# A stack of transformer blocks on one Trainium2 core: two weight remainders of the third attention move from VectorE to GpSimd

## The chip, the cores and the metric

The kernel runs on one core of one Trainium2 chip. The metric is the device time of one execution in microseconds (us); lower is better. All engines of the core work side by side and meet at semaphores only: TensorE (PE, with its weight loads shown apart as PEld), VectorE (DVE), ScalarE (ACT), GpSimd (POOL), and SyncE (SP), which only issues DMAs here.

## The reference

One sequence of 256 rows of width 1024 goes through four mixers in turn: stick-breaking attention and a gated conv MLP, forgetting attention and a gated conv MLP, and then the two layers of a second block. What the change touches is the first layer of that second block, a sliding-window attention with 16 query heads over 2 key heads and a gate ("the third attention"):

```python
def attention_mixer(h, positions, w_in, b_in, sinks, w_out, b_out):
    proj = h @ w_in + b_in
    q, k, v, z = jnp.split(proj, [ATTN_WIDTH, ATTN_WIDTH + KV_WIDTH, ATTN_WIDTH + 2 * KV_WIDTH], axis=-1)
    q = partial_rope(q.reshape(B, T, N_HEADS_2, HEAD_DIM_2), positions)
    k = partial_rope(k.reshape(B, T, N_KV_HEADS, HEAD_DIM_2), positions)
    v = v.reshape(B, T, N_KV_HEADS, HEAD_DIM_2)
    o = sliding_window_gqa(q, k, v, sinks)
    return (o * jax.nn.silu(z)) @ w_out + b_out
```

`sliding_window_gqa` is a softmax over a band of 128 keys with one learned sink per head; the layer after it is a gated recurrence. All of it is float32.

## The kernel before

**Weights.** All weight matrices lie in one stream of units, each 128 partitions by 2048 float32 (1 MB). SyncE loads unit after unit into three slots of `raw` (L391 to L397). TensorE multiplies in a rounded float32 format, so each unit is split in two: ScalarE writes the rounded part, `w_hi = round(raw)` (`split_hi`, L553 to L561), and VectorE the remainder, `w_lo = raw - w_hi` (`split_lo`, L1113 to L1117). A product then takes three matmuls, hi by hi, hi by lo and lo by hi (L1942 to L1944). `w_hi` and `w_lo` have three slots each. Four counters tie this together. `hi_done` counts finished rounded parts, `lo_done` finished remainders, `unit_done` the units that TensorE has used up, and `raw_loaded` the loads. SyncE loads unit u only when `lo_done` has reached u - 2, ScalarE rounds unit u only when `unit_done` has reached u - 2, and TensorE starts on unit u when `lo_done` has reached u + 1.

**The third attention.** Counted from zero, unit 98 holds its key and value weights, 99 to 102 its query weights, 103 to 106 the gate weights (`at_z`), 107 to 110 the output weights (`at_o`), and 111 is the first of the recurrence. The stage is written out by hand, one list of steps per engine: `window()` on ScalarE (L887), on VectorE (L1568) and on TensorE (L2569). The 16 heads go in eight pairs p = 0 to 7. For each pair TensorE makes the logits (L2356). VectorE adds the mask and takes the row maximum (`pair_max`, L1455), and makes `nmx` and `esink` from it (L1458, L1460). ScalarE takes the exponentials (L839, L843); VectorE sums and normalizes (`normalize`, L1468 to L1472). TensorE turns the probabilities (L2335), ScalarE copies them out (L852), and TensorE multiplies by the values (L2345, L2347). VectorE applies the gate (`gated`, L1589, after `gate_made`, L1583), and splits the result for the output product (`out_lo`, L1595, after ScalarE's L907). The pieces of the gate and output products lie between these steps on TensorE, so that it has work while a pair goes around the other engines. TensorE's logits of pair p wait for `gated` of pair p - 2, since they share PSUM banks.

VectorE does its remainders in fixed places in its list: unit 104 after the maximum of pair 0, unit 105 after `gated(0)`, 106 after the gate rows of unit 104, 107 after those of unit 105, and so on:

```python
                gated(0)
                split_to(u0 + 3)
...
                normalize(1, 3)
                gate_rows(2)
                split_to(u0 + 5)
```

Here `u0` is 103, so `split_to(u0 + 3)` brings the remainders up to unit 105 and `split_to(u0 + 5)` up to unit 107.

**GpSimd** makes constants and clears masked corners of the first two attentions (`affine_select`, L421). From then on it computes the small reciprocal square roots of the norms (L500, L506) and issues the loads of the norm gains (L494). Before the third attention its list reads `pre_scales(4)`, `next_gain(4)`, `post_scales(4)` (L528 to L530): the last waits for the norm that follows this attention.

Of the kernel before, what the change touches and what calls it, by code (L numbers as in the profile page):

```python
# [21 lines left out]
F32 = mybir.dt.float32  # L22
# [4 lines left out]
ALU = mybir.AluOpType  # L27
# [20 lines left out]
UNIT = 2048  # L48
RAW = 3
HL = 3  # L50
# [13 lines left out]
U0, E0 = {}, {}  # L64
# [24 lines left out]
def build(nc, stream, pvec, post_g, x_in, wf, bf, b_in, b_out, sinks, gnorm, pos, out):  # L89
    with ExitStack() as ctx:  # L90
        def sb(name, shape, dt=F32):
            return ctx.enter_context(nc.sbuf_tensor(name, shape, dt))

        def sem(name):
            return ctx.enter_context(nc.semaphore(name))

        raw = sb("raw", [P, RAW, UNIT])
        w_hi = sb("w_hi", [P, HL, UNIT], F32R)
        w_lo = sb("w_lo", [P, HL, UNIT], F32R)
# [35 lines left out]
        st = sb("st", [P, 12, 9, TT])  # L135
# [22 lines left out]
        last_rows_new = sem("last_rows_new")  # L158
        hi_done = sem("hi_done")
        lo_done = sem("lo_done")  # L160
        unit_done = sem("unit_done")
        chunk_freed_v = sem("chunk_freed_v")
        chunk_freed_s = sem("chunk_freed_s")
# [153 lines left out]
        def rows_wait(i, tt, c):  # L317

            if i in (1, 3):
                done = 2 * tt + c + 1  # L320
                return (rows_done, ROWS0[i] + done) if done < 4 else (unit_done, U0_END[i])
            return (rows_done, ROWS0[i] + c + 1) if tt == 0 else (unit_done, U0_END[i] - 1 + c)

# [89 lines left out]
        def _(pool):  # L413
# [77 lines left out]
            def next_gain(i):  # L491

                pool.wait_ge(h_new, 2 * TT * i)
                pool.dma_start(gbc[:, :], post_g[i].partition_broadcast(P)).then_inc(gbc_loaded, 16)  # L494

            def post_scales(i):

                for tt in range(TT):
                    pool.wait_ge(norm_mean, TT * i + tt + 1)
                    nc.gpsimd.tensor_tensor(st[:, 2 * i + 1, 4, tt:tt + 1], st[:, 2 * i + 1, 3, tt:tt + 1], minus_half[:, 0:1],  # L500
                                            ALU.pow).then_inc(norm_scale, 1)

            def pre_scales(i):

                pool.wait_ge(pre_mean, i + 1)
                nc.gpsimd.tensor_tensor(st[:, 2 * i, 4, :], st[:, 2 * i, 3, :], minus_half[:, :], ALU.pow).then_inc(row_scale, TT)  # L506
# [20 lines left out]
                post_scales(i)  # L527
            pre_scales(4)  # L528
            next_gain(4)
            post_scales(4)  # L530
            pre_scales(5)
            next_gain(5)
# [12 lines left out]
        def _(act):  # L545
# [34 lines left out]
            def split_half(u, i):  # L580

                cols = slice(1024 * i, 1024 * i + 1024)
                if i == 0:
                    assert u == nsplit[0]
                    act.wait_ge(raw_loaded[u % RAW], 16 * whole_loads(u))
                    act.wait_ge(unit_done, u - HL + 1)
                nc.scalar.activation(w_hi[:, u % HL, cols], raw[:, u % RAW, cols], ACT.Copy).then_inc(hi_done if i else half_hi, 1)
                if i:
                    nsplit[0] = u + 1

            def early_quarter(u, q):

                cols = slice(512 * q, 512 * q + 512)
                if u < EARLY:
                    act.wait_ge(quarter_loaded[4 * u + q], 16)
                elif q == 0:
                    act.wait_ge(raw_loaded[u % RAW], 16 * whole_loads(u))
                nc.scalar.activation(w_hi[:, u, cols], raw[:, u, cols], ACT.Copy).then_inc(hi_done if q == 3 else quarter_hi, 1)
                nsplit[0] = u + 1
# [9 lines left out]
            def pre(n, gain):  # L609


                for b in range(4):
                    if n % 2 and b == 1:
                        pre_square(n, 0, 1)
                    if n in SECOND and b in (1, 2):
                        pre_square(n, 1, b - 1)
# [8 lines left out]
                    if n == 0:  # L625
                        early_quarter(0, b)
                    if n in SECOND and b in (1, 2):
                        split_half(SECOND[n], b - 1)

            def pre_square(n, tt, c):  # L630

                if n == 0:
                    act.wait_ge(x_loaded[tt], 16)
                else:
                    act.wait_ge(h_new, 2 * TT * (n - 1) + 2 * tt + c + 1)
                nc.scalar.activation(junk(tt, c), h[:, tt, 512 * c:512 * c + 512], ACT.Square, scale=D ** -0.5,
                                     accum_out=st[:, 2 * n, c, tt:tt + 1]).then_inc(norm_ss, 1)
# [458 lines left out]
        def _(dve):  # L1096
# [8 lines left out]
            V = nc.vector  # L1105
# [7 lines left out]
            def split_lo(u, slot, raw_slot):  # L1113

                dve.wait_ge(hi_done, u + 1)
                V.tensor_tensor(w_lo[:, slot, :], raw[:, raw_slot, :], w_hi[:, slot, :].bitcast(F32),  # L1116
                                ALU.subtract).then_inc(lo_done, 1)  # L1117

            def split_to(n):
                for u in range(nsplit[0], min(n, NU)):  # L1120
                    split_lo(u, u % HL, u % RAW)
                nsplit[0] = max(nsplit[0], min(n, NU))

            def split_quarter(u, q):
# [9 lines left out]
            def split_half(u, i):  # L1134

                cols = slice(1024 * i, 1024 * i + 1024)
                if i:
                    dve.wait_ge(hi_done, u + 1)
                else:
                    assert u == nsplit[0]  # L1140
                    dve.wait_ge(half_hi, HALVED.index(u) + 1)
                V.tensor_tensor(w_lo[:, u % HL, cols], raw[:, u % RAW, cols], w_hi[:, u % HL, cols].bitcast(F32),
                                ALU.subtract).then_inc(lo_done if i else half_lo, 1)
                if i:
                    nsplit[0] = u + 1

            def early_quarter(u, q):

                cols = slice(512 * q, 512 * q + 512)
                if q == 3:  # L1150
                    dve.wait_ge(hi_done, u + 1)
                else:
                    dve.wait_ge(quarter_hi, 3 * u + q + 1)
                V.tensor_tensor(w_lo[:, u, cols], raw[:, u, cols], w_hi[:, u, cols].bitcast(F32),
                                ALU.subtract).then_inc(lo_done if q == 3 else quarter_lo, 1)
                nsplit[0] = u + 1
# [14 lines left out]
            def pre(n, gain):  # L1171
                for b in range(4):

                    if n in SECOND and b == 2:
                        pre_means(n)
# [6 lines left out]
                    if n == 0:  # L1182
                        early_quarter(0, b)
                    if n in SECOND and b in (1, 2):
                        split_half(SECOND[n], b - 1)

# [15 lines left out]
            def pre_means(n):  # L1202

                stats = st[:, 2 * n]
                dve.wait_ge(norm_ss, squares(2 * n, 1, 1))
                V.scalar_tensor_tensor(stats[:, 3, :], stats[:, 0, :], EPS, stats[:, 1, :], ALU.add, ALU.add).then_inc(pre_mean, 1)
# [94 lines left out]
            def conv_ffn(layer):  # L1301
# [45 lines left out]
                def chunk(j):  # L1347
                    if j < NJ - 1:
                        split_to(u0 + 3 * j + (3 if j else 4))
                    scaled(j, u0 + 3 * j + (2 if j == 0 else 0 if j == NJ - 1 else 1), j == 0)  # L1350
                    taps(j, j % 2)
                    if j < NJ - 1:
                        split_to(u0 + 3 * j + 4)
                    product(j, j % 2)
                    if j < NJ - 1:
                        split_to(u0 + 3 * j + 5)
                    if j == NJ - 1:
                        split_to(u0 + 3 * NJ)
                    gate_lo(j, j % 2)
# [1465 lines left out]


ROWS0 = [0, 2, 5, 7, 10, 12]
SECOND = {1: U0["ffn0"] + 1, 2: U0["fox_q"] + 1, 3: U0["ffn1"] + 1, 5: U0["rec_f"] + 1}
HALVED = list(SECOND.values())

# [78 lines left out]
```

## Time and profile before

| | |
|---|---|
| median of 3 runs | 866.98 us (866.67 to 867.33) |
| profiled execution, its own time | 867.6 us |
| its span in the trace | 865.9 us |
| PE busy | 854.0 us, 99% of the span |
| PEld busy | 751.9 us, 87% |
| DVE busy | 677.9 us, 78% |
| ACT busy | 524.0 us, 61% |
| POOL busy | 65.1 us, 8% |
| granted clock of TensorE | 0.999, mean over the span |

The profiled execution took 867.6 us, 0.6 us over the median of the three runs; its records cover 865.9 us of it, and the remaining 1.7 us lie around them. The third attention with its output product lies at about 640 to 720 us from the start of the span.

### The profile page before, as it was taken

What the parts mean: (1) busy time and instruction counts of PE and PEld (TensorE: products, weight loads), DVE (VectorE), ACT (ScalarE), POOL (GpSimd) and SP (SyncE); (2) the same over time, 40 slices, a digit from 0 to 9 for tenths busy, and PEclk for the clock granted to TensorE, in tenths of its full rate; (3) what the DMA queues carried; (4) which work ended last, traced back from release to release, by engine and by line L of the source; (5) the groups of instructions that cost most, each with busy time, mean ns of one, the idle gap of its engine ahead of it and who ended that gap; (6) DMA issues with size and microseconds to landing.
All of it is one profiled execution on the core that took longest, in us unless ns stands there. A gap on an engine that the chain in (4) does not pass through costs nothing.

```text
span 865.9 us, 15051 instructions
## 1 busy us (share of the span) xinstructions
PE 854.0 (99%) x5782; PEld 751.9 (87%) x5782; DVE 677.9 (78%) x994; ACT 524.0 (61%) x766; POOL 65.1 (8%) x128
## 2 busy tenths in 40 slices
PE   8999999999999999999999999999999999999997
PEld 8999889888888889999898888888888868998885
DVE  5767559897887987566589878888888877699774
ACT  6656557765665674667486655656746857542552
POOL 2354100000000010010010000000000001000010
PEclk9999999999999999999999999999999999999999
DMA  8545335645546445323456455455263244452511
GB/s 296 192 148 188 115 129 189 225 177 212 194 151 232 151 167 199 144 100 131 162 207 241 148 204 204 174 183 206 98 219 137 108 146 129 188 202 95 193 50 48
DMA packets 21976, 144.62 MB, mean 167 GB/s; under 512 B 2831, under 2 KB 3103, under 8 KB 5280
## 3 DMA queue, kind: packets, MB, share of 16 engines
q1 hardware_dynamic: 20448, 139.47, 44.5%
q0 software_dynamic: 1328, 4.32, 1.7%
q8 instruction: 40, 0.66, 0.3%
q14 instruction: 16, 0.13, 0.0%
q10 hardware_dynamic: 144, 0.04, 0.0%
HBM read 142.78 MB, written 1.05 MB: 166 GB/s over the span
## 4 chain that ended last, share of the span: by engine, by line
PE 86%; DVE 8%; ACT 2%; issue 2%; DMA 1%; POOL 0%; DVEq 0%; POOLq 0%; SPq 0%
PE psC L2034 15%; PE psC L1942 11%; PE psC L1944 11%; PE psC L1943 11%; PE psC L2037 8%; PE psD L1942 5%; PE psD L1944 5%; PE psD L1943 5%; DVE w_lo L1116 2%; PE psC L2064 2%; PE psC L2066 2%; PE psC L2073 2%; DVE arena L1330 2%; PE psD L2356 1%; PE psD L2736 1%
## 5 line engine op out<-in xcount | busy, mean ns | idle before, releaser
L1116 DVE TENSOR_TENSOR w_lo<-raw,w_hi 128x2048 fp32r<-128x2048 f32 x125 | 285.8, 2287 | 52.8 <-ACT w_hi L561 52.0
L561 ACT ACTIVATE w_hi<-raw 128x2048 fp32r<-128x2048 f32 x125 | 238.4, 1911 | 66.5 <-PE psC L1944 30.7
L2034 PE MATMUL psC<-xT,w_hi 128*128 128x512 f32 x640 | 200.8, 395 | 0.0
L2037 PEld LDWEIGHTS psC<-xT,w_lo 128*128 128x128 f32 x640 | 120.2, 188 | 28.3
L2037 PE MATMUL psC<-xT,w_lo 128*128 128x256 f32 x640 | 125.7, 278 | 0.0
L2034 PEld LDWEIGHTS psC<-xT,w_hi 128*128 128x128 f32 x640 | 98.6, 189 | 1.2
L1942 PE MATMUL psC<-xT,w_hi 128*128 128x256 f32 x320 | 91.6, 286 | 0.0
L1943 PE MATMUL psC<-xT,w_hi 128*128 128x256 f32 x320 | 90.5, 283 | 0.0
L1944 PE MATMUL psC<-xT,w_lo 128*128 128x256 f32 x320 | 90.5, 283 | 0.0
L1942 PE MATMUL psD<-w_hi,oT_hi 128*128 128x512 f32 x208 | 81.3, 391 | 0.6 <-DVE oT_lo L1344 0.6
L1943 PE MATMUL psD<-w_lo,oT_hi 128*128 128x512 f32 x208 | 81.0, 390 | 0.0
L1944 PE MATMUL psD<-w_hi,oT_lo 128*128 128x512 f32 x208 | 81.0, 389 | 0.0
L1330 DVE SCALAR_TENSOR_TENSOR arena<-arena,pv 128x254 f32<-128x254 f32 (+1 forms) x176 | 75.2, 479 | 5.4 <-DVE arena L1330 1.8
L1942 PE MATMUL psC<-w_hi,xT 128*128 128x256 f32 (+1 forms) x216 | 72.9, 338 | 0.9 <-issue 0.6
L1944 PE MATMUL psC<-w_hi,xT 128*128 128x256 f32 (+1 forms) x216 | 70.5, 327 | 0.0
L1943 PE MATMUL psC<-w_lo,xT 128*128 128x256 f32 (+1 forms) x216 | 70.5, 326 | 0.0
L706 ACT ACTIVATE arena<-arena,pv 128x256 f32<-128x256 f32 x88 | 47.8, 593 | 24.5 <-DVE arena L1320 24.5
L1942 PEld LDWEIGHTS psC<-xT,w_hi 128*128 128x128 f32 x320 | 61.3, 192 | 1.0 <-issue 1.0
L1943 PEld LDWEIGHTS psC<-xT,w_hi 128*128 128x128 f32 x320 | 61.3, 192 | 0.0
L1944 PEld LDWEIGHTS psC<-xT,w_lo 128*128 128x128 f32 x320 | 61.3, 192 | 0.0
L718 ACT ACTIVATE arena<-psC 128x512 f32<-128x512 f32 x40 | 23.8, 596 | 51.5 <-PE psC L2037 51.5
L1942 PEld LDWEIGHTS psC<-w_hi,xT 128*128 128x128 f32 x216 | 41.0, 190 | 6.7 <-issue 2.1
(338 smaller groups left out, 1538.0 us busy)
## 6 DMA issues: line engine op xcount, KB each, us to landing
raw<-stream SPq DMA_DIRECT2D x130, 1024.0 KB, 4.8
gbc<-post_g POOLq DMA_DIRECT2D x6, 512.0 KB, 4.7
h<-x_in SPq DMA_DIRECT2D x2, 512.0 KB, 4.4
raw<-stream SPq DMA_DIRECT2D x4, 256.0 KB, 6.2
out<-h SPq DMA_DIRECT2D x3, 256.0 KB, 2.0
arena<-b_in POOLq DMA_DIRECT2D x1, 640.0 KB, 5.9
out<-h SPq DMA_DIRECT2D x2, 128.0 KB, 2.0
pv<-pvec POOLq DMA_DIRECT2D x1, 176.0 KB, 4.7
```

What stands on the lines that cost most here:

```text
L561: nc.scalar.activation(w_hi[:, slot, :], raw[:, raw_slot, :], ACT.Copy).then_inc(hi_done, 1)
L706: ins = nc.scalar.activation(cv[:, par, g, a, :], xs[:, g, a, :], ACT.Identity, scale=pv[:, bass.ds(at + 2, 1)], bias=pv[:, bass.ds(at + 3 ...
L718: nc.scalar.activation(x_low[:, g], psC[:, at:at + 2, T:2 * T], ACT.Copy).then_inc(f["lower"], 1)
L1116: V.tensor_tensor(w_lo[:, slot, :], raw[:, raw_slot, :], w_hi[:, slot, :].bitcast(F32), ALU.subtract).then_inc(lo_done, 1)
L1330: ins = V.scalar_tensor_tensor(y, xs[:, g, a, 0:T - back], pv[:, bass.ds(at + 2 - back, 1)], y, ALU.mult, ALU.add)
L1942: MM(out, lhs[0], rhs[0], start=start, stop=False, skip_group_check=True)
L1943: MM(out, lhs[0], rhs[1], start=False, stop=False, skip_group_check=True)
L1944: return MM(out, lhs[1], rhs[0], start=False, stop=stop, skip_group_check=True)
L2034: MM(psC[:, up_bank(e, a), :], hi[:, k, a * P:a * P + P], xT[:, kk_, :, :].rearrange("p i t -> p (i t)"), start=(kk_ == 0), stop=False, sk ...
L2037: ins = MM(psC[:, up_bank(e, a), 0:T], lo[:, k, a * P:a * P + P], xT[:, kk_, 0, :], start=False, stop=(kk_ == KT - 1), skip_group_check=True)
L2064: MM(out(a), hi[:, k, a * P:a * P + P], xt[0][:, kk_, :], start=(kk_ == 0 and a % 2 == 0), stop=False, skip_group_check=True)
L2066: MM(out(a), lo[:, k, a * P:a * P + P], xt[0][:, kk_, :], start=False, stop=False, skip_group_check=True)
```

## The change

GpSimd gets two units of weight remainders, 105 (the third gate unit) and 107 (the first output unit). It waits for `hi_done` of the unit and then subtracts in eight operations of 256 columns. The last one counts up a new semaphore, `pool_lo`. VectorE no longer subtracts for these two units: at the same places in its list it waits for `pool_lo` and counts up `lo_done` with a memset of two columns of `st` that nothing else uses. TensorE, SyncE and ScalarE have the lists they had.

```diff
+        pool_lo = sem("pool_lo")
...
             pre_scales(4)
             next_gain(4)
+            for u in POOL_LO:
+                pool.wait_ge(hi_done, u + 1)
+                for at in range(0, UNIT, 256):
+                    cols = slice(at, at + 256)
+                    ins = nc.gpsimd.tensor_tensor(w_lo[:, u % HL, cols], raw[:, u % RAW, cols], w_hi[:, u % HL, cols].bitcast(F32),
+                                                  ALU.subtract)
+                ins.then_inc(pool_lo, 1)
             post_scales(4)
...
             def split_to(n):
                 for u in range(nsplit[0], min(n, NU)):
-                    split_lo(u, u % HL, u % RAW)
+                    if u in POOL_LO:
+                        dve.wait_ge(pool_lo, POOL_LO.index(u) + 1)
+                        V.memset(st[:, POOL_LO.index(u), 2, :], 0.0).then_inc(lo_done, 1)
+                    else:
+                        split_lo(u, u % HL, u % RAW)
                 nsplit[0] = max(nsplit[0], min(n, NU))
...
 ROWS0 = [0, 2, 5, 7, 10, 12]
+POOL_LO = [U0["at_z"] + 2, U0["at_z"] + 4]
```

Two places in the lists of the engines show it. Line numbers of the changed kernel are higher, by one in GpSimd's part before the insertion and by 12 in VectorE's part behind `split_to`. The first place is GpSimd's list between the norm ahead of the third attention and the one behind it. Before:

```order
L506 TENSOR_TENSOR st<-st,minus_half 128x2 [waits pre_mean]
L494 DMA gbc<-post_g 128x1024 [waits h_new]
L500 TENSOR_TENSOR st<-st,minus_half 128x1 [waits norm_mean] x2
L506 TENSOR_TENSOR st<-st,minus_half 128x2 [waits pre_mean]
L494 DMA gbc<-post_g 128x1024 [waits h_new]
```

and now:

```order
L507 TENSOR_TENSOR st<-st,minus_half 128x2 [waits pre_mean]
L495 DMA gbc<-post_g 128x1024 [waits h_new]
L535 TENSOR_TENSOR w_lo<-raw,w_hi 128x256 [waits hi_done]
L535 TENSOR_TENSOR w_lo<-raw,w_hi 128x256 x7
L535 TENSOR_TENSOR w_lo<-raw,w_hi 128x256 [waits hi_done]
L535 TENSOR_TENSOR w_lo<-raw,w_hi 128x256 x7
L501 TENSOR_TENSOR st<-st,minus_half 128x1 [waits norm_mean] x2
```

Sixteen operations stand where GpSimd went straight to the wait for the next norm.

The second place is VectorE's list from the exponentials of pair 1 to the maximum of pair 2. Before:

```order
L1468 TENSOR_TENSOR sums<-sums,esink 128x4 [waits win_exp]
L1469 RECIPROCAL rsum<-sums 128x4 [waits dve_step]
L1472 TENSOR_TENSOR arena<-arena,rsum 128x2x128 [waits dve_step]
L1472 TENSOR_TENSOR arena<-arena,rsum 128x2x256
L1583 SCALAR_TENSOR_TENSOR hn<-arena,hn 128x512 [waits gate_tanh]
L1589 SCALAR_TENSOR_TENSOR arena<-psD,hn 128x256 [waits gate_made,win_out]
L1116 TENSOR_TENSOR w_lo<-raw,w_hi 128x2048 [waits hi_done]
L1455 ISA arena,mx<-psD,mask_window 128x128 [waits win_logit]
```

and now:

```order
L1480 TENSOR_TENSOR sums<-sums,esink 128x4 [waits win_exp]
L1481 RECIPROCAL rsum<-sums 128x4 [waits dve_step]
L1484 TENSOR_TENSOR arena<-arena,rsum 128x2x128 [waits dve_step]
L1484 TENSOR_TENSOR arena<-arena,rsum 128x2x256
L1595 SCALAR_TENSOR_TENSOR hn<-arena,hn 128x512 [waits gate_tanh]
L1601 SCALAR_TENSOR_TENSOR arena<-psD,hn 128x256 [waits gate_made,win_out]
L1131 MEMSET st 128x2 [waits pool_lo]
L1467 ISA arena,mx<-psD,mask_window 128x128 [waits win_logit]
```

The subtraction of 2048 columns has become a memset of two behind a wait for GpSimd; nothing else has moved. Unit 107 is the same exchange, between the gate rows of unit 105 and the maximum of pair 4.

## Rows read from the trace of the kernel before

**Rows 1.** Busy time, share of the span and instructions, from the page's first part.
```profile
PE 854.0 (99%) x5782; PEld 751.9 (87%) x5782; DVE 677.9 (78%) x994; ACT 524.0 (61%) x766; POOL 65.1 (8%) x128
```

**Rows 2.** Busy time by stretch: the sum from 652 to 722 us, then the mean.
```profile
sum 70.00, PE 69.06 PEld 55.28 DVE 58.36 ACT 45.68 POOL 1.10; mean PE 17.27 PEld 13.82 DVE 14.59 ACT 11.42 POOL 0.28
```

**Rows 3.** Timeline of PE: start, us, engine, line, operation, tiles, [idle before and releaser].
```profile
665.14 0.38 PE L2356 MATMUL psD<-kT,qT 64*128 64x128 f32 x2 [0.50 <-DVE arena L1589]
```

**Rows 4.** Chain that ended last, in order of time: start, us, what.
```profile
653.85 2.20 DVE w_lo L1116
656.36 1.03 DVE arena L1472 x2
...
664.65 0.44 DVE arena L1589
```

**Rows 5.** Timeline of DVE between the maximum and the normalizing of pair 0.
```profile
652.17 0.16 DVE L1458 SCALAR_TENSOR_TENSOR nmx<-mx,arena 128x4 f32<-128x4 f32 x1
652.36 0.16 DVE L1460 TENSOR_TENSOR esink<-nmx,arena 128x4 f32<-128x4 f32 x1
652.44 1.40 DVE L1548 SCALAR_TENSOR_TENSOR arena<-psC,st,arena 128x512 f32<-128x512 f32 x2
...
655.96 0.15 DVE L1468 TENSOR_TENSOR sums<-sums,esink 128x4 f32<-128x4 f32 x1
```

**Rows 6.** Timeline of ACT: the rounded parts of units 105 and 107.
```profile
650.13 1.91 ACT L561 ACTIVATE w_hi<-raw 128x2048 fp32r<-128x2048 f32 x1 [3.93 <-PE psC L1944]
...
670.69 1.90 ACT L561 ACTIVATE w_hi<-raw 128x2048 fp32r<-128x2048 f32 x1
```

**Rows 7.** Timeline of DVE: the remainders of units 105 and 107.
```profile
665.00 2.28 DVE L1116 TENSOR_TENSOR w_lo<-raw,w_hi 128x2048 fp32r<-128x2048 f32 x1
...
680.79 2.29 DVE L1116 TENSOR_TENSOR w_lo<-raw,w_hi 128x2048 fp32r<-128x2048 f32 x1
```

**Rows 8.** Timeline of POOL: its last record before the third attention and the next.
```profile
628.84 0.59 POOL L494 DMA_DIRECT2D gbc<-post_g  x1
718.46 0.56 POOL L500 TENSOR_TENSOR st<-st,minus_half 128x1 f32<-128x1 f32 x1 [89.03 <-DVE st L1169]
```

**Rows 9.** Groups of POOL by form: count, busy us, mean ns, idle before and releasers.
```profile
L421 POOL TENSOR_SCALAR_AFFINE_SELECT arena<-arena 128x256 f32<-128x256 f32 x48 | 19.0, 425 | 130.7 <-ACT arena L829 78.4 <-DVE arena L1401 34.2 <-ACT arena L792 18.1
...
L421 POOL TENSOR_SCALAR_AFFINE_SELECT arena<-arena 128x2048 f32<-128x2048 f32 x2 | 4.0, 2004 | 0.1
```

**Rows 10.** DVE and POOL side by side: two lines' shortest, median and longest ns; timelines.
```profile
L1411 DVE CAST oT_hi<-arena x6: 559/648/740, 30.5 to 83.1; 128x768 fp32r<-128x768 f32 x6
...
L1412 DVE TENSOR_TENSOR oT_lo<-arena,oT_hi x6: 958/996/1039, 31.1 to 83.9; 128x768 fp32r<-128x768 f32 x6
...
48.55 0.69 DVE L1418 TENSOR_TENSOR oT_lo<-psC,oT_hi 128x512 fp32r<-128x512 f32 x1 [4.27 <-ACT oT_hi L797]
49.16 2.28 DVE L1116 TENSOR_TENSOR w_lo<-raw,w_hi 128x2048 fp32r<-128x2048 f32 x1
...
49.26 2.34 POOL L421 TENSOR_SCALAR_AFFINE_SELECT mask_level<-mask_level 128x64 int8<-128x64 int8 x1
...
83.00 0.41 POOL L421 TENSOR_SCALAR_AFFINE_SELECT arena<-arena 128x256 f32<-128x256 f32 x1
...
83.36 0.72 POOL L421 TENSOR_SCALAR_AFFINE_SELECT arena<-arena 128x256 f32<-128x256 f32 x1
...
83.08 0.74 DVE L1411 CAST oT_hi<-arena 128x768 fp32r<-128x768 f32 x1 [0.87 <-POOL arena L421]
83.86 1.04 DVE L1412 TENSOR_TENSOR oT_lo<-arena,oT_hi 128x768 fp32r<-128x768 f32 x1
```

**Rows 11.** Around unit 107: DVE normalizing pair 3, PE turning pair 3, PE's last wait.
```profile
679.12 1.03 DVE L1472 TENSOR_TENSOR arena<-arena,rsum 128x256 f32<-128x256 f32 x2
...
682.77 0.87 PE L2335 MATMUL psD<-ident,arena 128*128 128x128 f32 x6
...
705.26 0.87 PE L2335 MATMUL psD<-ident,arena 128*128 128x128 f32 x6 [0.42 <-DVE arena L1472]
```

## The prediction

> **What bounds the kernel now.** The page's first part comes first: PE is busy for 854.0 us, 99% of the span, VectorE for 78% and GpSimd for 8% [rows 1]. A cheaper VectorE can only give back time in which PE stands still. So the next view is the busy time by stretch: from 652 to 722 us, the 70 us in which the two units are split and used, PE is busy for 69.06 [rows 2]. Its idle time there is 0.94 us. The timeline of PE shows where most of it is. 0.50 us lie ahead of the logits of pair 2 at 665.14, which wait for VectorE's `gated(0)` (L1589) [rows 3]. 0.42 us lie ahead of the turning of pair 6 at 705.26, which waits for VectorE's normalizing [rows 11].
>
> The chain of work that ended last says more about the first of these. Between 652 and 665 us it doesn't run over PE but over VectorE: the remainder of unit 104, the normalizing of pair 0, and at last `gated(0)` at 664.65, which lets PE go on [rows 4]. In that stretch VectorE has no slack at all, and whatever delays it delays the end.
>
> When do the new operations run? GpSimd has nothing to do between 629.4 and 718.46 [rows 8], so it starts on a unit as soon as ScalarE has rounded it. For unit 105 that is 650.13 + 1.91 = 652.04, and for unit 107 it is 670.69 + 1.90 = 672.59 [rows 6]. VectorE comes to them only at 665.00 and 680.79 [rows 7]. The first eight operations thus fall exactly into the stretch in which VectorE carries the chain.
>
> **What is taken away.** Two subtractions of 2.28 and 2.29 us leave VectorE [rows 7]. Both lie behind `gated(0)`, so neither shortens the way to 665.14. What can come out of them is at most PE's idle time behind that point, 0.94 - 0.50 = 0.44 us [rows 2, 3]. Nearly all of it is the 0.42 at 705.26. Behind unit 107 VectorE's list waits for PE's logits of pairs 4, 5 and 6 in turn, so what it gained has gone by then, and between the last of these and 705.26 stands the remainder of unit 110, which VectorE keeps. I cost this relief at 0. The two memsets that replace the subtractions are two columns wide; they cost nothing on PE's path.
>
> **What an operation on GpSimd costs.** No row shows a two-input subtraction there. The nearest are operations with one input: 0.41 us for 256 columns alone, 0.36 from one start to the next (83.00 to 83.36) [rows 10], and 2.00 us for 2048 [rows 9]. That is (2.00 - 0.41) / 1792 = 0.89 ns for a column. If the second input is read after the first, it adds 256 x 0.89 ns = 0.23 us, which makes 0.59 from start to start and 4.7 us for a unit. The lower bound is the one-input spacing, 0.36; the upper is two one-input operations one after the other, 0.77 with the first alone. I take 0.59, between them, because it scales the same loop by the data it has to read.
>
> The Trainium skill, GPSIMD Engine Reference, section "Performance versus the Vector engine", gives 4497 ns for a 2048-column float32 `tensor_tensor` on GpSimd and says to keep elementwise work on VectorE. By it an eighth would be 0.56 us and the result below some 0.2 us smaller; no run so far shows the figure.
>
> **What the two engines do to each other.** Rows 10 have it in both directions. VectorE's cast (L1411) takes 559 ns undisturbed, and 740 where it starts at 83.08, inside GpSimd's operation of 83.00. GpSimd's next one, issued at 83.36, then takes 0.72 us instead of 0.41: it had to let the cast finish. VectorE's subtraction behind it (L1412, two inputs in SBUF) takes 1.04 instead of 0.96. And a small GpSimd operation that starts at 49.26, 0.10 us into a remainder of 2.28 us, lasts 2.34 us. So one of them stands still until the other's whole instruction is over. A VectorE instruction with one input from PSUM isn't touched: L1418 takes 0.69 us in the midst of GpSimd's mask operations [rows 10].
>
> The Trainium skill, SBUF — State Buffer, section "Who interferes with whom", has this as a rule: a VectorE instruction with two SBUF inputs and a GpSimd instruction that reads SBUF shut each other out for a whole instruction. By this rule GpSimd's subtractions aren't work beside VectorE's but partly in front of it; the rows above agree.
>
> **The sum for unit 105.** GpSimd starts at 652.1 and runs an operation every 0.59 us, and I let the two engines take turns. From each wait I take off 0.1 us, because the waits in rows 10 (0.18 and 0.08 us) are that much shorter than the overlap of the records. VectorE's instructions with two SBUF inputs are met in this order [rows 4, 5]:
> - `nmx` at 652.17 waits for the first operation: 0.4.
> - `esink`, which comes after it through a semaphore, waits for the second: 0.45.
> - The two L1548 read PSUM and run free for 1.3 us, while operations 3 to 5 pass.
> - The remainder of unit 104 (653.76) meets one of them half way: 0.3. GpSimd stands still for its 2.28 us.
> - `sums` (655.96) finds the sixth operation in front: 0.5.
> - The two L1472 (656.36) meet the seventh and eighth: 0.25 and 0.45.
>
> That is 2.35 us, say 2.4, and the eight operations end near 659.5, in time for 665. The whole delay goes through. The maximum of pair 1, ScalarE's exponentials and tanh, `gate_made(0)` and `gated(0)` follow one on another, and PE, which already waits 0.50 us there, starts the logits of pair 2 2.4 us later. Behind it PE is bound by its own work, so nothing is won back. With a spacing of 0.36 the same walk gives 0.7 us, with 0.77 it gives 3.6.
>
> **The sum for unit 107.** Here VectorE has room. PE turns pair 3 at 682.77, and the normalizing that it needs ends at 679.12 + 1.03 = 680.15 [rows 11], 2.6 us earlier; the missing remainder of unit 105 adds some 0.6, as pair 3's maximum no longer starts behind PE's logits. Eight collisions cost some 2.3 us, spread over instructions of which only some stand ahead of that point. I cost them at 0; at 0.77 us an operation they could reach 4, and cost PE up to 1. GpSimd needs 4.7 us and the 2.28 of unit 106's remainder, until 679.6, and VectorE asks at about 680.8, so the new wait isn't the later one.
>
> **Sum**: 0 + 2.4 + 0 = +2.4 us. Against the profiled execution of 867.6 that is 870.0; against the median of the runs, 866.98, which lies 0.6 lower, it is 869.4.
>
> **Rivals.** A measurement of this kernel can tell about 0.2%, 1.7 us, from no change.
> - *GpSimd yields.* If VectorE's next instruction goes first whenever both wait, or if an operation takes only 0.36 us, the small instructions lose 0.1 or 0.2 us each instead of 0.45. The delay is then 0.7 to 1.6 us, and the time 867.7 to 868.6: no change that can be told. This decides below a delay of 1.7 us. For it speaks the one-input spacing; against it speaks that `nmx` and `esink` come one by one through semaphores, so that GpSimd finds a gap each time. 0.28.
> - *The relief pays.* If the engines hardly met and the relief reached 705.26, PE would win up to 0.44 us: 866.5. Faster by over 1.7 us would need more than all 0.94 us of idle time in the stretch [rows 2]. 0.03 for that.
> - *Unit 107 hurts too.* With operations of 0.77 us the first unit costs 3.6 and the second up to 1: 871.6. If one took over (665.07 - 652.1) / 8 = 1.6 us, VectorE would also wait for `pool_lo`, and the time would pass 875. It lies within the chance for slower, with 0.15.
>
> **How the numbers follow.** The forecast has 0.54 and the worse rival 0.15, so slower by over 0.2% has 0.69, within it 0.28, faster 0.03. The predicted time is that of the likeliest case, 869.4. The range goes from 867.2, which takes in most of the first rival, to 871.8, the two upper bounds together. Outside remain the relief, most of it, and the case of much slower operations.
>
> **What would show it.** In the profile after: 16 subtractions on POOL with starts about 0.6 us apart where undisturbed, one of each eight stretched over 2.3 us by a remainder on VectorE; `nmx`, `esink`, `sums` and L1472 of pair 0 longer by 0.3 to 0.5 us; PE idle ahead of the turning of pair 0 and of the logits of pair 2, some 2.5 us in sum more than before; the idle 0.42 at the turning of pair 6 still there; memsets behind `pool_lo` without a wait. If `nmx` and `esink` keep their 0.16 us the step on the collisions is wrong. If they grow and the logits of pair 2 still start near 665.1, the step that gives VectorE no slack is wrong.

## The result, and the profile after

| | before | after |
|---|---|---|
| median of 7 runs each | 866.98 us (866.67 to 867.68) | 870.07 us (869.8 to 870.49) |
| ratio, with its 95% interval | | 1.0034 (1.0025 to 1.0044) |
| profiled execution, its own time | 867.6 us | 869.8 us |
| span in the trace | 865.9 us | 868.1 us |

The change makes the kernel slower, by 3.1 us between the medians and by 2.2 to 3.8 us by the interval. The busy times of the page's first part, against [rows 1]:

```profile
PE 853.1 (98%) x5782; PEld 750.7 (86%) x5782; DVE 678.9 (78%) x994; ACT 524.3 (60%) x766; POOL 78.9 (9%) x144
```

VectorE has two subtractions of 2.29 us less to do and is busy for 1 us *more* than before. Its records contain the time in which it was held up. The timeline of PE has these waits between 652 and 712 us, against [rows 3, 11] (columns as there):

```profile
659.13 0.88 PE L2347 MATMUL psD<-ident,arena 128*128 128x128 f32 x6 [2.00 <-DVE arena L1484]
...
667.35 0.93 PE L2368 MATMUL psD<-kT,qT 64*128 64x128 f32 x8 [1.22 <-DVE arena L1601]
...
707.47 0.87 PE L2347 MATMUL psD<-ident,arena 128*128 128x128 f32 x6 [0.42 <-DVE arena L1484]
```

Before there were 0.50 us ahead of the logits of pair 2, and now there are 2.00 ahead of the turning of pair 0 and 1.22 ahead of those logits. The 0.42 us at the turning of pair 6 are unchanged. The first two waits come to 2.72 us more than the 0.50 before. The kernel loses 2.95 us in this stretch, as the next paragraph works out, and the other 0.23 us stand in no wait of the timeline.

Two distances on PE measure a stage better than the span does, since the time at which the stage begins varies by up to 1.3 us from one profiled execution to another (649.22 us here, 650.56 in the kernel `no_relief` below): from the first matmul of pair 0's logits to that of pair 2's, and from there to the end of the span. Before they are 665.14 - 649.96 = 15.18 and 865.9 - 665.14 = 200.76 us. After they are 667.35 - 649.22 = 18.13 and 868.1 - 667.35 = 200.75 us. So all of the loss, 2.95 us, lies in the stretch of unit 105, and nothing is lost or won behind it. The execution profiled before began this stage 0.74 us later than the one after, which is why the two spans differ by 2.2 us only.

The chain that ended last shows VectorE carrying this stretch, as in [rows 4], now with stretched pieces:

```profile
651.42 0.73 DVE nmx L1470
...
652.17 0.67 DVE esink L1472
652.85 1.32 DVE arena L1560 x2
654.17 2.21 DVE w_lo L1124
656.38 0.63 DVE sums L1480
...
657.24 1.83 DVE arena L1484 x2
659.07 0.74 DVE arena L1532
```

And this is what GpSimd does meanwhile: its operations by start and length, the line of its subtractions (shortest, median and longest ns), and both units as a whole:

```profile
652.09 1.43 POOL L535 TENSOR_TENSOR w_lo<-raw,w_hi 128x256 fp32r<-128x256 f32 x2
652.79 0.73 POOL L535 TENSOR_TENSOR w_lo<-raw,w_hi 128x256 fp32r<-128x256 f32 x1
...
654.20 2.78 POOL L535 TENSOR_TENSOR w_lo<-raw,w_hi 128x256 fp32r<-128x256 f32 x1
...
L535 POOL TENSOR_TENSOR w_lo<-raw,w_hi x16: 726/742/2782, 651.4 to 681.4; 128x256 fp32r<-128x256 f32 x16
...
651.39 8.28 POOL L535 TENSOR_TENSOR w_lo<-raw,w_hi 128x256 fp32r<-128x256 f32 x8 [22.71 <-ACT w_hi L569]
...
673.80 8.38 POOL L535 TENSOR_TENSOR w_lo<-raw,w_hi 128x256 fp32r<-128x256 f32 x8 [14.14 <-ACT w_hi L569]
```

An undisturbed operation takes 0.70 us from start to start (652.09 to 652.79). The one that starts at 654.20, just behind VectorE's remainder of unit 104, takes 2.78: it waits for that remainder. The other meetings cost VectorE. The last two cost GpSimd something as well: beside VectorE's two L1484 its operations take 0.91 and 1.18 us instead of 0.73.

VectorE's timeline around unit 107 shows the same collisions; in this kernel nothing is lost behind pair 2:

```profile
674.03 2.66 DVE L1124 TENSOR_TENSOR w_lo<-raw,w_hi 128x2048 fp32r<-128x2048 f32 x1
...
677.95 0.74 DVE L1470 SCALAR_TENSOR_TENSOR nmx<-mx,arena 128x4 f32<-128x4 f32 x1
678.73 0.65 DVE L1472 TENSOR_TENSOR esink<-nmx,arena 128x4 f32<-128x4 f32 x1
...
679.63 1.22 DVE L1595 SCALAR_TENSOR_TENSOR hn<-arena,hn 128x512 f32<-128x512 f32 x1
...
681.82 1.24 DVE L1484 TENSOR_TENSOR arena<-arena,rsum 128x256 f32<-128x256 f32 x2
...
683.74 0.06 DVE L1131 MEMSET st<- 128x2 f32 x1
685.10 0.29 DVE L1467 CUSTOM_DVE_ANT_0 arena<-psD,mask_window 128x128 f32<-128x128 f32 x1 [1.30 <-PE psD L2368]
```

Undisturbed, these five take 2.29, 0.16, 0.16, 0.69 and 1.03 us, so VectorE loses 0.37 + 0.58 + 0.49 + 0.53 + 0.21 = 2.18 us here. In the place of unit 107's subtraction stands the memset of 0.06 us, and behind it VectorE is 1.30 us early for pair 4.

### The profile page after: what moved, and what is told of

Same layout as the page of the kernel before. It is cut to its first block, busy times and chain, and to the rows that moved or that the text cites. A ratio compares the mean times of both kernels' runs of the same rounds, so it can differ in the third digit from the quotient of the medians.

```text
span 868.1 us, 15067 instructions
## 1 busy us (share of the span) xinstructions
PE 853.1 (98%) x5782; PEld 750.7 (86%) x5782; DVE 678.9 (78%) x994; ACT 524.3 (60%) x766; POOL 78.9 (9%) x144
## 4 chain that ended last, share of the span: by engine, by line
PE 88%; DVE 6%; ACT 2%; issue 2%; DMA 1%; POOL 0%; SPq 0%; POOLq 0%; DVEq 0%
PE psC L2046 15%; PE psC L1954 12%; PE psC L1956 11%; PE psC L1955 11%; PE psC L2049 8%; PE psD L1954 5%; PE psD L1955 5%; PE psD L1956 5%; PE psC L2076 2%; PE psC L2078 2%; PE psC L2085 2%; DVE w_lo L1124 2%; PE psD L2368 1%; PE psD L2748 1%; DVE arena L1342 1%
## 5 line engine op out<-in xcount | busy, mean ns | idle before, releaser
L1124 DVE TENSOR_TENSOR w_lo<-raw,w_hi 128x2048 fp32r<-128x2048 f32 x123 | 281.5, 2289 | 52.3 <-ACT w_hi L569 51.5
L501 POOL TENSOR_TENSOR st<-st,minus_half 128x1 f32<-128x1 f32 x12 | 6.7, 554 | 472.9 <-DVE st L1181 472.9
```

## The experiments

Theory: a meeting of the two engines costs VectorE the rest of one GpSimd operation, and PE pays where VectorE carries the chain. Eleven kernels test it. Each was run five times or more beside runs of the kernel before, and a difference in us is between these medians. The distances are those defined above, each from one profiled execution. The first is 15.18 in all four kernels in which nothing touches it (before, `only_107`, `write_only`, `no_relief_107`). The second is good to 0.1 us, since the span is given in tenths.

| kernel | median | before, beside it | ratio (95%) | pair 0 to pair 2 | pair 2 to end |
|---|---|---|---|---|---|
| before | 866.98 | | | 15.18 | 200.76 |
| the change | 870.07 | 866.98 | 1.0034 (1.0025 to 1.0044) | 18.13 | 200.75 |
| only_105 | 870.79 | 867.46 | 1.0039 (1.0026 to 1.0053) | 18.34 | 200.73 |
| only_107 | 867.89 | 867.46 | 1.0004 (0.9995 to 1.0013) | 15.18 | 201.04 |
| no_relief | 873.37 | 867.46 | 1.006 (1.0046 to 1.0073) | 18.13 | 203.91 |
| write_only | 867.69 | 867.46 | 1.0002 (0.9993 to 1.0011) | 15.18 | 200.81 |
| no_relief_107 | 869.18 | 867.49 | 1.0026 (1.0017 to 1.0035) | 15.18 | 202.38 |
| early_104_pool | 870.87 | 867.49 | 1.0042 (1.0028 to 1.0055) | 16.25 | 203.15 |
| early_104 | 869.49 | 867.49 | 1.0019 (1.001 to 1.0028) | 14.61 | 203.59 |
| one_op | 874.67 | 867.49 | 1.0088 (1.0074 to 1.0102) | 20.34 | 202.54 |
| only_104 | 867.87 | 867.22 | 1.0007 (0.9998 to 1.0017) | 15.54 | 200.78 |
| early_104_pool_b | 868.41 | 867.22 | 1.0013 (1.0004 to 1.0022) | 16.25 | 200.74 |
| ops_128 | 871.52 | 867.22 | 1.0043 (1.0029 to 1.0057) | 17.95 | 202.25 |

### Which unit costs

```diff
-POOL_LO = [U0["at_z"] + 2, U0["at_z"] + 4]
+POOL_LO = [U0["at_z"] + 2]
```

> GpSimd makes the remainder of unit 105 alone; unit 107 is VectorE's again. Theory (collisions while VectorE carries the chain, all of it at unit 105): the whole loss stays, +2.9 to +3.1 us against the kernel before, near 870.0. Rival A (both units cost about the same): half of it, near 868.5. Rival B (the loss comes from unit 107, whose collisions reach the turning of pair 3): 867.0.

and with `U0["at_z"] + 4` alone:

> GpSimd makes the remainder of unit 107 alone. Theory: its collisions (some 2.5 us on VectorE, a stretched nmx, esink and gate_made of pair 3) fall into VectorE's slack of 2.6 us ahead of the turning of pair 3, and the relief is worth nothing: 866.7 to 867.3, no difference. Rival A (half of the loss each): 868.5. Rival B: 870.0.

Measured: +3.3 us for unit 105 alone and +0.4 for unit 107 alone, the latter within its interval of no difference. The first theory holds, with a loss 0.2 us above its range, and both rivals fall. The distance from pair 0 to pair 2 has the whole loss for unit 105 and is unchanged, 15.18, for unit 107. Behind pair 2 `only_107` is 0.28 us longer than the kernel before, some 0.2 of it as small pieces of idle time of PE between 680 and 695 us. The profiled execution of `only_105` has something of its own besides. Behind the 2.00 us for which PE waits there, the granted clock falls (busy by stretch as in [rows 2], with length, PE, PEld, DVE, ACT, POOL, clock; then PE's timeline):

```profile
658.00:660.00 2.00, 0.26 (x2) 0.26 (x3) 2.00 (x3) 0.00 (x0) 2.00 (x3) 1.00 0.98 279
660.00:664.00 4.00, 4.00 (x24) 3.63 (x24) 3.61 (x18) 1.72 (x6) 0.27 (x1) 0.57 0.29 123
...
659.74 1.15 PE L2347 MATMUL psD<-ident,arena 128*128 128x128 f32 x6 [2.00 <-DVE arena L1484]
```

For most of the stretch from 660 to 664 PE has half its clock (0.57 on the mean, between the levels of 2.4 and 1.2 GHz). It then comes to pair 2 without the wait of 1.22 us: PE works through the time in which it would have waited for VectorE, and the slow clock costs only the 0.21 us by which 18.34 exceeds 18.13.

### Is it the collisions, and are they worth more than the relief?

GpSimd subtracts as in the change, and VectorE subtracts the units again behind its wait:

```diff
                     if u in POOL_LO:
                         dve.wait_ge(pool_lo, POOL_LO.index(u) + 1)
-                        V.memset(st[:, POOL_LO.index(u), 2, :], 0.0).then_inc(lo_done, 1)
-                    else:
-                        split_lo(u, u % HL, u % RAW)
+                    split_lo(u, u % HL, u % RAW)
```

> GpSimd subtracts as in the change, but VectorE, after its wait for pool_lo, subtracts both units once more, as before the change: the collisions are there, the relief isn't. Theory (collisions are the loss, the relief is worth nothing): as the change, 870.0, within 0.3 us. Rival (the relief is worth something and hides a larger loss): slower than the change by what it is worth, up to 872 if both subtractions of 2.3 us counted.

Measured: +5.9 us, not 3. For the two units together the theory falls, and the rival, that the relief hides a larger loss, is nearer; the time lies even over its bound. The stretch of unit 105 behaves as expected, 18.13 us as in the change, so that loss is the collisions' and the relief of unit 105 takes nothing off it. But 3.15 us more are lost behind pair 2 (203.91 - 200.76). On PE's timeline and the busy time by stretch:

```profile
696.91 0.80 PE L1952 MATMUL psC<-w_hi,oT_hi 128*128 128x512 f32 x1 [1.37 <-DVE w_lo L1124]
...
697.00:700.40 3.40, 3.40 (x10) 2.19 (x12) 1.62 (x11) 2.42 (x10) 0.00 (x0) 0.51 0.68 222
```

PE waits 1.37 us for the remainder of unit 108, and runs at about half clock (0.51) for the next 3.4. The slower clock isn't in every execution: one of the five had a granted clock of 1.000 over the span and took 872.1 us, 4.6 over the kernel before. So my claim that unit 107's relief is worth nothing was too simple: it covers what unit 107's own collisions cost. The next kernel does this for unit 107 alone:

> GpSimd subtracts unit 107 alone, and VectorE, behind its wait, subtracts it once more. Theory (unit 107 cost nothing in the change because VectorE's missing 2.28 us there pay for its own collisions of some 2.2 us; with both units and no relief PE waited 1.4 us for the remainder of unit 108 and ran at half clock for 3.4 us behind it): now VectorE is 2 us late from pair 4 on, PE waits up to 1.4 us for unit 108 or less where this kernel's slack of pair 2 is larger: +0.5 to +3 us. Rival (unit 107 has slack of its own, and the extra 2.9 us of the kernel without relief come from the two units together): no more than 0.4 us over the kernel before, as with relief.

Measured: +1.7 us, with the same wait of 1.37 us, in this execution without a fall of the clock:

```profile
693.25 0.50 PE L1952 MATMUL psC<-w_hi,oT_hi 128*128 128x512 f32 x1 [1.37 <-DVE w_lo L1124]
```

The first expectation holds and its rival falls. With the relief taken away, the collisions of unit 107 cost 202.38 - 200.76 = 1.62 us. The place at which they are paid isn't the turning of pair 3 but unit 108. In the kernel before its remainder ends at 691.59, and PE begins to use it at 691.73 (timelines of VectorE and PE before):

```profile
689.30 2.29 DVE L1116 TENSOR_TENSOR w_lo<-raw,w_hi 128x2048 fp32r<-128x2048 f32 x1
...
691.73 0.50 PE L1942 MATMUL psC<-w_hi,oT_hi 128*128 128x512 f32 x1
```

These are 0.14 us. In `no_relief_107` VectorE comes to this remainder 1.73 us later than before, counted from the logits of pair 2, and PE has to wait. In the change the missing subtraction of unit 107 makes up for it.

### What do the engines share?

GpSimd's subtractions become three passes of memsets, and VectorE, behind its wait for them, subtracts both units itself (shown against the change, without the subtraction's arguments and VectorE's part):

```diff
-                for at in range(0, UNIT, 256):
-                    cols = slice(at, at + 256)
-                    ins = nc.gpsimd.tensor_tensor(...)
-                ins.then_inc(pool_lo, 1)
+                for i in range(3):
+                    for at in range(0, UNIT, 256):
+                        ins = nc.gpsimd.memset(w_lo[:, u % HL, at:at + 256].bitcast(F32), 0.0)
+                    ins.then_inc(pool_lo, 1)
+                    pool.wait_ge(pool_lo, 3 * POOL_LO.index(u) + i + 1)
```

> GpSimd's subtractions are replaced by memsets of the same slot, three passes of eight with 256 columns each, some 7 us of work that writes SBUF and reads nothing; VectorE waits for it and subtracts both units itself. Theory (what VectorE's two-input instructions and GpSimd share is the reading of SBUF): no instruction of VectorE gets longer, 866.7 to 867.3, as the kernel before. Rival (any GpSimd work at that time holds VectorE up, or the semaphore traffic does): nmx, esink and sums of pair 0 grow by 0.2 us or more each, 868 to 870.

Measured: +0.2 us, no difference. GpSimd is at work all through pair 0's steps, and none of them is longer:

```profile
651.76 6.37 POOL L535 MEMSET w_lo<- 128x256 f32 x24 [22.66 <-ACT w_hi L569]
...
651.82 0.16 DVE L1468 SCALAR_TENSOR_TENSOR nmx<-mx,arena 128x4 f32<-128x4 f32 x1
652.02 0.17 DVE L1470 TENSOR_TENSOR esink<-nmx,arena 128x4 f32<-128x4 f32 x1
```

So neither GpSimd's writing nor the semaphores hold VectorE up in this stretch. What is left is its reading of SBUF; a memset is also another kind of operation than a subtraction, and no kernel here separates the two. The Trainium skill, SBUF — State Buffer, section "Who interferes with whom", says of VectorE's instructions with two SBUF inputs that they contend with a GpSimd instruction that reads SBUF and not with one that only writes it; these traces agree (0.16 us for `nmx` beside the memsets, 0.72 beside the subtractions).

### How long is one held off?

One subtraction of 2048 columns instead of eight, and in a later kernel sixteen of 128:

```diff
-                for at in range(0, UNIT, 256):
-                    cols = slice(at, at + 256)
+                for at in range(0, UNIT, UNIT):
+                    cols = slice(at, at + UNIT)
```

> Each of the two units is one subtraction of 2048 columns on GpSimd, not eight of 256. Theory (whoever starts first holds the other off for a whole instruction): nmx of pair 0 waits for all of unit 105, some 5 us, and nothing behind it waits; for unit 107 either the remainder of unit 106 waits 5 us or GpSimd waits for it. PE then loses 5 us at pair 0 and up to 3 more at unit 106 or through the clock: 872 to 876. Rival (the two engines share column by column, so that only the sum of the columns counts): 870.5, as the change.

> The change with sixteen operations of 128 columns for each unit. From 0.70 us start to start at 256 columns and 4.59 us for 2048 an operation of 128 takes about 0.43. Theory (each of VectorE's two-input instructions waits for at most one operation, so the loss is the number of meetings times what is left of one): more meetings, since the six small rope operations are met too, each of 0.3 us instead of 0.5: +3 to +4 us, not better than the change. Rival (finer operations halve each wait and with it the loss): +1.5 to +2 us.

Measured: +7.2 us for one operation, of which 5.16 lie between pair 0 and pair 2 (20.34 - 15.18) and 1.78 behind (202.54 - 200.76), as expected. GpSimd's operation, VectorE's `nmx` of four columns, and PE:

```profile
651.79 4.59 POOL L535 TENSOR_TENSOR w_lo<-raw,w_hi 128x2048 fp32r<-128x2048 f32 x1 [22.70 <-ACT w_hi L569]
...
651.83 4.57 DVE L1470 SCALAR_TENSOR_TENSOR nmx<-mx,arena 128x4 f32<-128x4 f32 x1
...
661.52 0.88 PE L2347 MATMUL psD<-ident,arena 128*128 128x128 f32 x6 [3.98 <-DVE arena L1484]
```

An instruction of 0.16 us takes 4.57 because it comes 0.04 us too late. The engines don't share by column; one is held off for the other's whole instruction. Of the 5.16 us these 4.41 are VectorE's. Behind its wait of 3.98 us PE has a lower clock (0.54 from 662 to 665), and comes to pair 2 without a further wait, so the other 0.75 us go with the clock. At unit 107 the remainder of unit 106 meets GpSimd's operation and takes 6.51 us instead of 2.28, and PE waits for it for 0.99 us. The Trainium skill, GPSIMD Engine Reference, section "Performance versus the Vector engine", gives 4497 ns for an addition of 2048 float32 columns; the subtraction here takes 2% more, 4.59 us.

For sixteen operations: +4.3 us, no better than eight; the theory had +3 to +4. Each is 0.42 us from start to start (651.87 to 652.29), and the six rope operations, of which eight operations met one, are met as well (VectorE's timeline of `ops_128`):

```profile
651.90 0.43 DVE L1470 SCALAR_TENSOR_TENSOR nmx<-mx,arena 128x4 f32<-128x4 f32 x1
...
658.38 0.54 DVE L1532 TENSOR_TENSOR arena<-arena,cosin 128x128 f32<-128x128 f32 x1
658.84 0.54 DVE L1533 TENSOR_TENSOR arena<-arena,cosin 128x128 f32<-128x128 f32 x1
```

The first distance is 17.95, 0.18 us less than with eight operations; the second is 1.5 us longer, in an execution whose clock fell to half for 3.4 us behind a wait of 2.14 ahead of pair 2. So finer pieces change the collisions little, and what `ops_128` has over the change goes with the clock; its fastest execution is 2.5 us over the kernel before. The rival, half the loss (+1.5 to +2), falls.

### Does the place of VectorE in the chain matter?

The remainder of unit 104 is made ahead of pair 0's maximum, and the work on the bias rows, 1.8 us, moves behind unit 106 (`bias_rows_made()` holds the removed lines). First with the change:

```diff
-            split_to(U0["at_z"] + 1)
-            dve.wait_ge(bias_split, 1)
-            settle(V.tensor_scalar(two_rows, neg_ones[0:33, :], 0.0, None, ALU.mult))
...
+            split_to(U0["at_z"] + 2)
...
                 split_to(u0 + 4)
+                bias_rows_made()
```

> The change, and VectorE makes the remainder of unit 104 before the maximum of pair 0, in the place of its work on the bias rows (1.8 us), which moves behind the remainder of unit 106. Theory (the collisions cost only because VectorE carries the chain there): 2.28 us leave the chain, of which some 0.8 are lost again as waiting for ScalarE's exponentials; with all eight collisions of unit 105 there the delay at the logits of pair 2 is 0.3 to 1.0 us instead of 3: 867.8 to 868.5 where the kernel before has 867.5. Rival (the eight operations cost their time wherever VectorE stands, or PE loses it through the clock): 870 to 870.8, as the change.

Then the same move in the kernel before:

> The kernel before, with the same move of unit 104's remainder and the bias rows, nothing on GpSimd. Theory: the chain over VectorE between 652 and 665 us gets 1.4 us shorter, PE's idle 0.50 us ahead of the logits of pair 2 goes: -0.5 us. Rival (the 1.8 us that move behind unit 106 reach the turning of pair 3, slack 2.6 us): +0.0 to +0.5 us.

Measured: +3.4 and +2.0 us; as times, both expectations missed. The distances take them apart. In the kernel before the move shortens the first by 0.57 us (14.61), as expected, and the idle 0.50 us is gone. But 2.83 us are lost behind (203.59 - 200.76). The bias rows bring VectorE late to unit 108, for which PE waits 1.26 us:

```profile
692.43 0.51 PE L1946 MATMUL psC<-w_hi,oT_hi 128*128 128x512 f32 x1 [1.26 <-DVE w_lo L1116]
```

The rest goes with the clock, which is at half for 3.4 us behind this wait (0.53 from 693.0 to 696.4). The eleven runs of `early_104` show the same. Five have a granted clock of 0.999 or 1.000 over the span and take 867.98 to 868.47 us, some 0.8 over the kernel before; six have 0.996 or 0.997 and take 869.49 to 870.33. The median of +2.0 lies in the second group. By the first the move still isn't a gain: 1.26 us of waiting outweigh the 0.57 won.

With the change on top the first distance is 16.25, only 1.07 us over before instead of 2.95; I had expected 0.3 to 1.0. The other 2.4 us are lost at pairs 3 and 4, which now carry unit 107's collisions and the bias rows together; no kernel here tells what each alone would cost there (four waits of PE, of which the first two lie ahead of pair 2):

```profile
658.06 0.87 PE L2351 MATMUL psD<-ident,arena 128*128 128x128 f32 x6 [0.65 <-DVE arena L1484]
...
665.75 0.93 PE L2372 MATMUL psD<-kT,qT 64*128 64x128 f32 x8 [0.68 <-DVE arena L1601]
...
684.57 0.87 PE L2351 MATMUL psD<-ident,arena 128*128 128x128 f32 x6 [1.07 <-DVE arena L1484]
...
687.91 0.65 PE L2361 MATMUL psD<-arena,vt 128*64 128x256 f32 x4 [1.04 <-ACT arena L860]
```

So I put the bias rows where unit 105's subtraction had stood and left unit 107 to VectorE:

```diff
-POOL_LO = [U0["at_z"] + 2, U0["at_z"] + 4]
+POOL_LO = [U0["at_z"] + 2]
...
                 split_to(u0 + 3)
+                bias_rows_made()
```

> Unit 105 alone on GpSimd, the remainder of unit 104 made early as in the kernel early_104, but the bias rows' 1.8 us stand where unit 105's 2.28 us stood, not behind unit 106. Theory (the eight collisions of unit 105 now cost PE 0.8 us, as the two idle stretches of early_104_pool showed; its other 2.1 us came from the bias rows ahead of pair 3, which leave no slack for them): +0.6 to +1.1 us against the kernel before. Rival (the loss stays where GpSimd works): +3 us.

Measured: +1.2 us, just above the expectation, with the first distance again 16.25 and the second back at 200.74. The rival of +3 falls. Against the kernel before PE loses 1.07 us in the first stretch, but the move alone wins 0.57 there, so the eight operations cost 16.25 - 14.61 = 1.64 us, not 2.95. VectorE is held up for 2.47 us (`nmx` 0.56, `esink` 0.51, `sums` 0.58, the two L1484 0.82); the rope comes after GpSimd has finished. Of the 2.47, 0.83 don't reach PE: 0.39 go into a wait for ScalarE's exponentials of pair 1, which is 1.69 us in `early_104` and 1.30 here, and 0.44 into the time that `gated(0)` had to spare. So slack helps, as the theory has it, and the collisions that are left still cost more than the move wins. It still isn't faster than the kernel before.

Last, a unit whose relief lies on the chain itself:

> GpSimd makes the remainder of unit 104 alone, whose 2.28 us on VectorE stand inside the chain from pair 0 to the logits of pair 2 (unit 105's stand behind it). It starts at about 646.2. Theory (what counts is on which side of PE's wait the collisions and the relief lie): collisions with the remainder of unit 103, the bias rows, nmx and esink cost 1.8 to 2.5 us, the relief of 2.28 now lies on the same chain, and 0.5 us are absorbed by VectorE's idle time ahead of pair 0: -0.5 to +0.8 us. Rival (a unit on GpSimd costs its collisions wherever it is): +2 to +3 us.

The edit is `POOL_LO = [U0["at_z"] + 1]`. Measured: +0.65 us (interval -0.2 to +1.5), within the expectation; the rival of +2 to 3 falls. The first distance is 15.54, 0.36 over before. VectorE's timeline shows the bias rows' collisions and where `nmx` of pair 0 starts:

```profile
648.76 0.75 DVE L1770 TENSOR_SCALAR oT_lo<-neg_ones 33x128 fp32r<-33x128 f32 x1
649.54 1.35 DVE L1772 TENSOR_SCALAR oT_lo<-neg_ones 1x128 fp32r<-1x128 f32 x2
650.82 1.77 DVE L1773 SCALAR_TENSOR_TENSOR oT_hi<-arena,oT_hi 1x1024 fp32r<-1x1024 f32 x1
...
653.85 0.16 DVE L1470 SCALAR_TENSOR_TENSOR nmx<-mx,arena 128x4 f32<-128x4 f32 x1
```

In the kernel before the first three take 0.21, 0.45 and 1.21 us. With the remainder of unit 103 (2.54 us instead of 2.28) the collisions come to 2.26 us. They don't outweigh the relief by themselves. `nmx` starts 3.97 us behind the first logits instead of 2.21, 1.76 later, since VectorE's idle time ahead of pair 0 takes up the rest. But the relief of 2.28 us is worth only 1.40: from `nmx` to `sums` it is 2.39 us instead of 3.79, and now `sums` waits 0.70 us for ScalarE's exponentials. 1.76 - 1.40 is the 0.36. No version tried is faster than the kernel before; the most that the whole stretch holds is the 0.94 us of [rows 2].

## Why the prediction was right, and where it wasn't

- **What bounds the kernel.** Right. VectorE carries the chain from pair 0 to pair 2, and its delay of 2.95 us came out at the end in full (18.13 - 15.18, with 200.75 unchanged). `only_105` shows that unit 105 does it. `early_104_pool_b` shows what VectorE's lack of slack has to do with it: with some slack 1.64 of 2.47 us reach PE, without it all of 2.95. PE's waits grew by 2.72 us, where some 2.5 were forecast.
- **The cost of an operation.** Too small: 0.59 us against 0.70. The upper bound of 0.77 and the lower of 0.36 enclose it. The step that failed is the second input, which I priced at one more reading by the slope of the one-input rows, 0.89 ns a column and so 1.78 for two. From 0.70 us at 256 columns and 4.59 at 2048 (the latter alone) it is (4.59 - 0.73) / 1792 = 2.15 ns, with 0.73 for one alone.
- **What the engines do to each other.** Right in kind, and with it the sum for unit 105, 2.4 us against 2.95. Term by term: `nmx` 0.56 (forecast 0.4), `esink` 0.51 (0.45), the remainder of unit 104 nothing (0.3), `sums` 0.54 (0.5), the two of L1472 0.80 (0.7), and the first rope operation 0.54 (none). The longer operations were still not done when the rope came, and the remainder of unit 104 happened to start between two of them. That the sum is off by 0.6 us only is in part luck: the 0.3 too much for the remainder make up for part of what the operations' length and the rope add.
- **The sum for unit 107.** The number was right, 0, and in part by luck: one of its reasons was wrong. Collisions of 2.18 us (forecast 2.3) and GpSimd finished in time for VectorE's memset, without a wait. But I looked for the slack at the turning of pair 3. The place that decides is the remainder of unit 108, which had 0.14 us, and the relief that I costed at 0 is what pays there: without it the unit costs 1.6 us.
- **The relief at the end.** Right: 0.42 us of idle time at pair 6 stayed in every profile that has unit 110 on VectorE, that is in all of them.
- **The rivals.** GpSimd doesn't yield to the small instructions: `nmx`, `esink` and `sums` each lose most of an operation, 0.5 us and more. Beside the longer L1484 it is held up too, by 0.18 and 0.45 us, so the engines do take turns there. The relief paid nothing by itself. The worse case of operations of 0.77 us, with a loss at unit 107 too, didn't come: they take 0.70, and VectorE's memsets found both units finished.

## What to carry to other kernels

An engine that is idle for 92% of the span isn't free: before work goes to GpSimd, list VectorE's instructions in the same stretch that read SBUF through two inputs, count each meeting at the rest of one GpSimd operation, and see whether VectorE carries the chain there. Here 2.3 us of relief cost VectorE 2.2 to 3 us of collisions at each of the three units tried, and the split into eight operations only kept a loss of 7 us down to 3. And a relief has to lie ahead of the wait that it should shorten; behind it, it can at best pay for the damage done by its own transfer. Ahead of it, it is worth only what the next engine in the chain leaves of it: 1.40 of 2.28 us in `only_104`.

## What the runs showed of the hardware that I had not expected

- A meeting is priced by GpSimd's instruction, not VectorE's: four columns, 0.16 us alone, took 0.72 behind an operation of 256 columns and 4.57 behind one of 2048.
- Splitting finer than eight hardly helped: sixteen operations of 0.42 us lost 2.77 us between the pairs, eight of 0.70 lost 2.95.
- A `tensor_scalar` with a single SBUF input was held up too, from 0.21 to 0.75 us (L1770 in `only_104`), as the cast in [rows 10] was. The kernels don't tell whether its form or its partitions matter.
- Behind some waits of PE the granted clock was at half, the 1.2 of the two levels 1.2 and 2.4 GHz, for 3.4 us, and behind others of like length it wasn't. It fell behind waits of 1.26 us (`early_104`), 1.37 (`no_relief`), 2.00 (`only_105`), 2.14 (`ops_128`) and 3.98 (`one_op`), and stayed up behind 2.00 (the change) and 1.37 (`no_relief_107`). Between `no_relief` and `no_relief_107`, which wait 1.37 us at the same place, it makes 203.91 - 202.38 = 1.53 us. The runs of `early_104` split into two groups by their clocks, and their medians, 868.25 and 869.82, differ by 1.6 us. The eleven runs of `no_relief_107` fall into two groups as well, 868.68 to 869.18 and 870.18 to 871.03; their clocks, 0.998 or 0.999 against 0.997 or 0.998, point the same way but don't separate them. So a wait of 1.3 us can cost about twice its length, where no later wait hides it as in `only_105`.
